# First-group attention in place, log gates summed in the projection, tile 0 routed and chosen before the rest of its group

## The reference, cut to what matters

```python
h = rms_norm(x, norm1_g)
rq, rk, rv, rg, fq, fk, fv, ff = split(h @ w_in)      # 7 groups of 512 columns, 8 gate columns
logf = log_sigmoid(ff + b_f)
ro = retention(rotary(rq), rotary(rk), rv)            # 8 heads of 64
c = cumsum(logf)                                      # along tokens
fo = softmax(fq @ fk.T / 8 + c_q - c_k, causal) @ fv  # 8 heads of 64
x = x + concat(rms(ro) * silu(rg), rms(fo)) @ w_out
# PEER: 8 heads, 2 x 128 keys each, 16 experts of 16384 per head and token
q = rms_norm(x) @ wq
v1, i1 = top_k(q1 @ keys1, 16); v2, i2 = top_k(q2 @ keys2, 16)
cv, ci = top_k(v1[:, None] + v2[None, :], 16)         # 16 x 16 candidates per head
e = i1[ci // 16] * 128 + i2[ci % 16]; g = softmax(cv)
x = x + sum_k g_k * gelu(x . u[e_k]) * v[e_k]         # 128 experts per token, 1024 + 1024 values each
```

## Time and profile before

| | |
|---|---|
| median of three runs | 4024.57 us (4021.61 to 4029.34) |
| the profiled execution's own time | 4017.62 us |
| its span, first to last instruction | 4015.8 us |
| TensorE busy | 2392.5 us (60%) |
| VectorE busy | 2507.4 us (62%) |
| ScalarE busy | 474.8 us (12%) |
| GpSimd busy | 1397.8 us (35%) |
| mean granted TensorE clock | 0.748 |
| gather queue, share of the 16 DMA engines' span | 72.9% (1208.03 MB) |
| all DMA | 1361.03 MB, mean 339 GB/s |

### The profile page before, as it was taken

One profiled execution on the slowest core, in us unless ns is written; L12 is line 12 of the kernel. 1 busy time (PEld: TensorE's weight loads), 2 busy tenths in 40 slices (PEclk: granted clock), 3 DMA queues, 4 the chain that ended last, 5 costly groups with the idle time before them and its releaser, 6 DMA issues.

```text
span 4015.8 us, 34713 instructions
## 1 busy us (share of the span) xinstructions
PE 2392.5 (60%) x11906; PEld 984.7 (25%) x11906; DVE 2507.4 (62%) x6235; ACT 474.8 (12%) x1311; POOL 1397.8 (35%) x1257
## 2 busy tenths in 40 slices
PE   7999867838847665855726746684334334334333
PEld 3456333413313222322402322231001001001000
DVE  3226211789656655888886656689887555555555
ACT  1001121211102201101111211010001000000000
POOL 0001100026434433433343434344444444444443
PEclk9988957969968887876767878796666656556556
DMA  3010342079999998999999999999999999999998
GB/s 112 21 37 22 122 161 100 6 287 418 387 417 419 414 420 360 411 389 409 407 412 418 411 411 420 378 411 412 419 410 419 419 419 418 417 419 418 420 417 371
DMA packets 252929, 1361.03 MB, mean 339 GB/s; under 512 B 33857, under 2 KB 54153, under 8 KB 105297
## 3 DMA queue, kind: packets, MB, share of 16 engines
q0 software_dynamic: 165888, 1208.03, 72.9%
q1 hardware_dynamic: 84560, 148.45, 10.1%
q10 hardware_dynamic: 2304, 2.32, 0.2%
HBM read 1328.37 MB, written 30.35 MB: 338 GB/s over the span
## 4 chain that ended last, share of the span: by engine, by line
DMA 37%; PE 20%; DVE 15%; POOL 7%; issue 6%; ACT 1%; SPq 1%; POOLq 0%; DVEq 0%; ACTq 0%
DMA M<-in_peer_uv,M 35%; PE yp L1952 11%; POOL M L1524 7%; DVE M L2210 6%; PE ab L1905 2%; PE c L1884 1%; DMA M<-qts_scratch 1%; DVE strips L2232 1%; DVE exg L2227 1%; PE d L1768 1%; PE ab L1745 1%; DMA qts_scratch<-M 1%; PE d L1884 1%; PE ef L1940 1%; DVE gel L2219 1%
## 5 line engine op out<-in xcount | busy, mean ns | idle before, releaser
L1524 POOL DMA_INDIRECT M<-in_peer_uv,M x1152 | 1308.9, 1136 | 1937.5 <-PE yp L1952 1499.2
L2210 DVE SCALAR_TENSOR_TENSOR M<-M 128x1024 f32<-128x1024 f32 x1152 | 1410.4, 1225 | 838.7 <-DMA M<-in_peer_uv,M 805.3
L1952 PE MATMUL yp<-M,strips 128*32 128x512 f32 x4608 | 905.4, 927 | 1301.6 <-DVE strips L2232 1263.3
L1952 PEld LDWEIGHTS yp<-M,strips 128*32 128x32 f32 x4608 | 161.3, 145 | 1924.0 <-DVE strips L2232 1509.0
L1706 ACT ACTIVATE gel<-gel 128x4 f32<-128x4 f32 x288 | 59.2, 206 | 2113.1 <-DVE gel L2221 2076.6
L1905 PE MATMUL ab<-M 128*128 128x512 f32 x576 | 263.8, 609 | 1.3 <-ACT M L1662 1.3
L411 PE MATMUL z<-M 128*128 128x512 f32 x432 | 188.4, 593 | 0.9 <-PEq L104 0.9
L1905 PEld LDWEIGHTS ab<-M 128*128 128x128 f32 x576 | 109.1, 196 | 142.3 <-issue 140.7
L1785 PE MATMUL ab<-M 128*128 128x512 f32 x288 | 133.4, 613 | 13.1 <-issue 10.0
L2232 DVE SCALAR_TENSOR_TENSOR strips<-gel,exg 128x128 f32<-128x128 f32 x288 | 84.0, 292 | 59.1 <-ACT gel L1706 49.2
L1745 PE MATMUL ab<-M 64*128 64x512 f32 (+3 forms) x192 | 96.7, 618 | 27.7 <-DMA M<-qts_scratch 22.3
(11 more groups left out here) (232 smaller groups left out, 2578.1 us busy)
## 6 DMA issues: line engine op xcount, KB each, us to landing
M<-in_peer_wq SPq DMA_DIRECT2D x12, 2048.0 KB, 28.1
M<-in_w_in SPq DMA_DIRECT2D x9, 2048.0 KB, 8.6
M<-in_peer_uv,M POOLq DMA_INDIRECT x1152
M<-in_w_out SPq DMA_DIRECT2D x24, 512.0 KB, 25.4
M<-in_x_prompt SPq DMA_DIRECT2D x16, 512.0 KB, 10.2
x_scratch<-M SPq DMA_DIRECT2D x9, 512.0 KB
xts_scratch<-M SPq DMA_DIRECT2D x9, 512.0 KB, 35.9
M<-xts_scratch SPq DMA_DIRECT2D x9, 512.0 KB
```

Of the source, the lines that this page charges most:

```text
L1524: nc.gpsimd.indirect_dma_start(ring[n % NR], None, a["peer_uv"], bass.IndirectOffsetOnAxis(ap=idxH[:, t % 6, s // 4, s % 4:s % 4 + 1], axis=0)
L1952: last = nc.tensor.matmul(yp[32 * j:32 * j + 32, 512 * c:512 * c + 512], strips[:, n % 2, j, :], ring[(4 * n + j) % NR][:, D + 512 * c:D + ...
L2210: nc.vector.scalar_tensor_tensor(out=row, in0=row, scalar=1.0, in1=xrep[:, s % 4, :], op0=ALU.mult, op1=ALU.mult, accum_out=dots[:, t % 2, ...
```

## The change

1. In the second projection the log gates of the prompt are transposed behind step 3 and those of the samples behind step 5; ScalarE copies them at steps 4 and 6, VectorE sums them ahead of step 5, and SyncE stores `csd` and `lft` ahead of step 6. `lgfT`, `ones0` and `csum0` move to parts of the value and key regions that this phase leaves unused.
2. The attention of group 0 reads `qT`, `kT` and `vn` where the projection left them, and the retention outputs where the retention left them; the loads of `kTg`, `vg`, `fq` and `mix` are gone for g = 0. The tail begins with the decay rows of heads 0 and 1.
3. The weights follow later decay rows: w_out's first four chunks behind the row of head 2, the other four behind head 3, wq blocks 0 and 1 behind heads 4 and 5, the routing keys behind head 6.
4. Group 0 routes tile 0 first (i = 0 to 3), then block by block for tiles 1 and 2. In the plan the first top 16 of i = 4 needs tile 0's choice to be complete. Gather 4 waits for `s_mm` 8. The routing keys of group 0 are split in two places, so that blocks 2 and 3 lie outside the ring.
5. The plan's model changes: `rscore` needs the SyncE part of the last `hxt`, which costs 32 us instead of 6 for groups 1 and 2 (the keys are loaded there), and two of three SyncE slots of a tile count as ready four dots later.

```diff
-        lgfT = Hreg[0:NH, 7040:7040 + TILES * P]
+        lgfT = M[0:NH, 28160:28160 + TILES * P]
+        ones0, csum0 = M[0:NH, 29312:29312 + NP_TOK], M[0:NH, 32768:32768 + NP_TOK]
...
+                        if with_ff and n == 6:
+                            sp.wait_ge(c_done, 1)
+                            sp.dma_start(a["csd"], csum0).then_inc(out_done, 16)
+                            sp.wait_ge(ffT, 2)
+                            sp.dma_start(a["lft"], lgfT[:, NP_TOK:]).then_inc(out_done, 16)
+                            outs += 2
...
+                        if with_ff and n == 3:
+                            pe.wait_ge(ff_log, 1)
+                            for u in range(PT):
+                                last = nc.tensor.transpose(ffpt[:, u // 4, (u % 4) * P:(u % 4 + 1) * P], lgf[:, u, :], ident[:, :])
+                            last.then_inc(ft_done, 1)
+                        if with_ff and n == 5:
+                            pe.wait_ge(ffT, 1)
+                            nc.tensor.transpose(ffpt[:, 0, 0:P], lgf[:, ST, :], ident[:, :]).then_inc(ft_done, 1)
...
+                        if with_ff and n == 5:
+                            dve.wait_ge(ones_set, 1)
+                            dve.wait_ge(ffT, 1)
+                            nc.vector.tensor_tensor_scan(out=csum0, data0=ones0, data1=lgfT[:, 0:NP_TOK],
+                                                         initial=0.0, op0=ALU.mult, op1=ALU.add).then_inc(c_done, 1)
...
-                add(rest, ("load", g), sp=(55.0 if g else 12.0, *routed))
-                add(rest, ("loadq", g), sp=(40.0 if g else 15.0, *chosen))
+                add(rest, ("load", g), sp=(55.0 if g else 6.0, *routed))
+                if g:
+                    add(rest, ("loadq", g), sp=(40.0, *chosen))
...
-                            act=(1.4, ("pe", ("hxt", g, j))), sp=(6.0, ("act", ("hxt", g, j))))
+                            act=(1.4, ("pe", ("hxt", g, j))),
+                            sp=(32.0 if g and j == GT - 1 else 6.0, ("act", ("hxt", g, j))))
...
-                            add(rest, ("rscore", g, i), pe=(1.4, ("act", ("rturn", g, i)), *bank("D", "act", ("rscore", g, i))),
+                            add(rest, ("rscore", g, i), pe=(1.4, ("act", ("rturn", g, i)), ("sp", ("hxt", g, GT - 1)),
+                                                              *bank("D", "act", ("rscore", g, i))),
                                 act=(0.7, ("pe", ("rscore", g, i)), *old))
+                        first = [("dve", ("rcand", 0, 0, CAND - 1))] if g == 0 and i == 5 and p == 0 else []
                         if i >= 1:
-                            add(rest, ("rtop", g, i - 1, p), dve=(1.15, ("act", ("rscore", g, i - 1))))
+                            add(rest, ("rtop", g, i - 1, p), dve=(1.15, ("act", ("rscore", g, i - 1)), *first))
...
-                    top = ("rtop", g, 4 * i + 3 if g == 0 else n - GT + i, 4)
+                    top = ("rtop", g, 3 if g == 0 and i == 0 else n - GT + i, 4)
...
-            return (i % 4, i // 4) if g == 0 else (i // GT, i % GT)
+            if g:
+                return i // GT, i % GT
+            return (i, 0) if i < 4 else ((i - 4) // 2, 1 + i % 2)
...
-                need = (P * t - 1, P * t - 1, P * t + 3)[k] if i else -1
+                need = (P * t + 3, P * t + 3, P * t + 3)[k] if i else -1
...
-            keys4 = M[:, 16384:18432].rearrange("p (s i n) -> p s i n", s=4, i=4)
+            keys4 = [M[:, o:o + 1024].rearrange("p (s i n) -> p s i n", s=2, i=4) for o in (16384, 34304)]
...
                     elif kind == "decay":
                         h = arg[0]
                         sp.wait_ge(ttr_done, FIRST[g] + (h - 1) * len(tiles_of(g)))
                         load_decay(NH * g + h)
+                        if g == 0 and h in (2, 3):
+                            load_wout(0, range(4 * h - 8, 4 * h - 4))
+                        elif g == 0 and h in (4, 5):
+                            load_wq(0, h - 4)
+                        elif g == 0 and h == 6:
+                            for b in range(4):
+                                sp.dma_start(keysT(0, b), a["keys_t"][:, 4 * b:4 * b + 4, :]).then_inc(key_in[b], 16)
...
                     if n == 4:
-                        pool.wait_ge(s_mm, 4 * GT)
+                        pool.wait_ge(s_mm, 8)
...
+                    rows_q, rows_k = (fq[:, :, i * P:(i + 1) * P], kTg) if g else (qT[:, :, t * P:(t + 1) * P], kT)
...
-                nc.vector.tensor_tensor_scan(out=csum0, data0=ones0, data1=lgfT0[:, 0:NP_TOK],
-                                             initial=0.0, op0=ALU.mult, op1=ALU.add).then_inc(c_done, 1)
```

More of the change, by code:

```diff
@@ L421, in _ @@
                             turn(n)
[L422 to L430, removed]
                 @block.scalar
@@ L452, in _ @@
                     for n, (g, t) in enumerate(steps):
+                        if with_ff and n == 4:
+                            act.wait_ge(ft_done, 1)
+                            nc.scalar.copy(lgfT[:, 0:NP_TOK], ffpt[:, :, :].rearrange("h a n -> h (a n)")).then_inc(ffT, 1)
+                        if with_ff and n == 6:
+                            act.wait_ge(ft_done, 2)
+                            nc.scalar.copy(lgfT[:, NP_TOK:], ffpt[:, 0, 0:P]).then_inc(ffT, 1)
                         if g in (RV, FV):
@@ L469, in _ @@
                             evacuate(n)
[L470 to L475, removed]
                 @block.gpsimd
@@ L479, in _ @@
                     steps_done = 0
+                    if with_ff:
+                        nc.gpsimd.memset(ones0, 1.0).then_inc(ones_set, 1)
                     for m, n in enumerate(normed):
@@ L910, in fox @@
                         add(rest, ("decay", g, h + 1), sp=(11.0 if g else 2.5, ("dve", ("foxs", g, last))))
-                wait = [("sp", ("load", g)), ("sp", ("loadq", g))] if n == FIRST[g] else []
+                wait = [("sp", ("load", g)), ("sp", ("loadq", g))] if g and n == FIRST[g] else []
                 old = [("act", ("foxs", g, n - 2))] if n - 2 >= FIRST[g] else []
                 free = [("pe", ("foxp", g, n - 3))] if n - 3 >= FIRST[g] else []
-                cb = [("sp", ("decay", g, h))] if h >= 2 else []
+                cb = [("sp", ("decay", g, h) if h >= 2 else ("load", g))]
                 add(rest, ("foxs", g, n),
@@ L1085, in work_ready @@
                         return None
-                    empty = done.get(("pe", ("rscore", 0, 4 * GT - 1)))
+                    empty = done.get(("pe", ("rscore", 0, 7)))
                     if i >= 4 and empty is None:
@@ L1304, in rows, with load_wout @@
                         a[name + "_s"][0].rearrange("b n h d -> (b n) (h d)")
-                def load_wout(g):
-                    for k in range(KC):
+                def load_wout(g, chunks=range(KC)):
+                    for k in chunks:
                         sp.dma_start(wout(g)[:, k, :], a["w_out"][0, k * P:(k + 1) * P, :]).then_inc(w_in[k], 16)
@@ L1444, in load_xTn @@
                     sp.dma_start(xTn.rearrange("p k n -> p (k n)"), a["xts"][t]).then_inc(xTn_in, 16)
-                sp.wait_ge(c_done, 1)
-                sp.dma_start(a["csd"], csum0).then_inc(cs_out, 16)
-                sp.dma_start(a["lft"], lgfT0[:, NP_TOK:]).then_inc(lf_out, 16)
+                for step in due["sp"][0][:1]:
+                    front(step)
                 sp.dma_start(grow[:, :], a["norm2_g"].partition_broadcast(P)
@@ L1452, in _ @@
                 for t in range(TILES):
-                    for step in due["sp"][3 * t]:
+                    for step in due["sp"][3 * t][0 if t else 1:]:
                         front(step)
@@ L1527, in gather @@
                     ).then_inc(uv_in[n % NR], 16)
-                nc.gpsimd.memset(ones0, 1.0).then_inc(ones_set, 1)
                 for n in range(P * TILES):
@@ L1744, in scores @@
                         w = min(512, width - c)
-                        nc.tensor.matmul(s[:, c:c + w], fq[b0:b0 + 64, r, i * P:(i + 1) * P],
-                                         kTg[b0:b0 + 64, r, c:c + w], start=True, stop=c + w < width)
+                        nc.tensor.matmul(s[:, c:c + w], rows_q[b0:b0 + 64, r], rows_k[b0:b0 + 64, r, c:c + w], start=True, stop=c + w < width)
                     nc.tensor.matmul(s[:, t * P:width], identb[:, :], maskq[:, :], start=False, stop=True
@@ L1767, in values @@
                     for j in range(t + 1):
-                        last = nc.tensor.matmul(Dk[b0:b0 + 64, 0:P], vg[:, j, h * HD:(h + 1) * HD], pT[:, n % 2, j, :],
+                        last = nc.tensor.matmul(Dk[b0:b0 + 64, 0:P], (vg if g else vn)[:, j, h * HD:(h + 1) * HD], pT[:, n % 2, j, :],
                                                 start=(j == 0), stop=(j == t))
```

40 lines of the change are left out of this document (15 added, 25 removed).

## The result

The changed kernel takes 3983.09 us (median of four runs, 3978.03 to 3989.30), against 4026.45 us (4021.61 to 4029.34) for the kernel before. The ratio is 0.9897, 95% interval 0.988 to 0.9913: 43 us gained where 75 were forecast. The profiled execution has a span of 3982.5 us and a time of its own of 3984.28 us. The pair of profiled executions differs by 33.3 us only, since that of before lies 8.8 us under its median and that of after 1.2 us above its own. In that of after the phases that the change does not touch also ended 5.1 us later.

The account below looks back on a forecast made before the run. The gather stream on the DMA engines sets the end by its start, bytes and holes. Starting 65 us earlier, plus 18 for holes, less a 7 us wait, makes 76, taken as 75: 4024.6 - 75 = 3950 us, range 3928 to 3982.

Parts of the forecast that it names:

- The projection's end: Second projection, before the tail: early transposes make the last stores about 1.3 us later, bounds 0 to +1.4.
- The attention: Group 0's attention: no wait for queries or late decay rows, ending at 591.4, a gain of 23.5 us, bounds 17 to 25.
- the rival of the high clock: Group 0's attention: TensorE's clock stays high, saving about 25 us more, total 3925 us; chance 0.12.
- Choosing tile 0, and gather 4: Stream start: top 16 tasks moved behind tile 0's choice gain 29.4 us, gather 4 needing score 8 gains 11.8.
- Holes (part 5): First routing scores of groups 1 and 2: the plan's cost fills the waits for keys, gaining 18 us, bounds 0 and 18.
- The holes stay: Rival: the wait for the keys only moves to another step ahead of `add_v`, total 3962 us; chance 0.13.
- A new wait at tile 3: Gather 384, tile 3's first: ready at 1884, numbers at 1891, a wait of 7 us, bounds nothing to 37.
- The prediction's own sum: Start of group 1's front: eight remaining top 16 tasks, slowed by dots from about 777, end at 857.
- the prediction's argument that the choice would run faster: Gather 384: while GpSimd waits, VectorE has no dots, so the choice runs two to three times faster.
- The front of group 1 comes late: Rival: delayed projection of tiles 3 to 8 makes GpSimd wait at gather 384, total 3979 us; chance 0.15.

Follow-up runs that it names:

- Experiment 2: Changed kernel with group 0 routed tile by tile again, no early choice of tile 0, gather 4 waiting for score 12: 4006.47 us, ratio 0.9941.
- Experiment 5: Changed kernel without the early choice of tile 0 in the plan, new routing order and wait for score 8 kept: 4006.34 us, ratio 0.9947.
- Experiment 3: Changed kernel with the plan's new dependency and 32 us cost for the keys undone, SyncE slots kept: 3987.32 us, ratio 0.9898.
- experiment 4: Changed kernel with SyncE issuing the keys of groups 1 and 2 ahead of the last store and of wq block 1: 3963.73 us, ratio 0.9844.
- experiment 1: Changed kernel with tile 3 using tile 2's expert numbers and gates, so its gathers don't wait for its own: 3977.98 us, ratio 0.9877.
- experiment 7: The kernel of experiment 1 with twelve pieces of tile 3's choice left out: 3966.7 us, ratio 0.9843.
- experiment 6: The kernel of experiment 4 with the projection's first 2 MB of weights issued once group 0's last queries are made: 3955.63 us, ratio 0.9817.

## Why the prediction was right up to the stream, and wrong behind it

**The projection's end** was right: from the first of the 128x512 matmuls to the end of the last, 65.5 us before and 66.5 after, +1.0 for a forecast of 1.3.

**The attention** was right in size and in place. The first minimum started 3.1 us after the issue of its decay row (519.41), at net 517.4 (518.2 forecast), there was no later wait for a row, and the last `fout` ended at net 591.4. (The forecast's 591.4 goes back to the start of the last `fout`, 614.91; start against start it is net 590.8.) The clock stayed at its low level as the forecast took it, so the rival of the high clock is out; three windows of after:

```profile
530.00:535.00 5.00, 5.00 (x18) 2.82 (x17) 0.57 (x2) 1.89 (x8) 0.00 (x0) 0.50 0.90 330
560.00:565.00 5.00, 4.65 (x17) 2.96 (x16) 1.04 (x6) 2.26 (x8) 0.00 (x0) 0.50 0.67 174
590.00:595.00 5.00, 4.21 (x17) 2.75 (x17) 0.00 (x0) 1.64 (x5) 0.00 (x0) 0.50 0.02 3
```

Experiment 2 confirms the price by itself: about 22 us.

**Choosing tile 0, and gather 4** were right: choice end net 761.4 (762), gather 0 net 766.4 (767), gather 4 6.3 us behind it (within 7). Experiment 5 measures the early choice alone at 29.4 us of start.

**Failed: "Holes (part 5)".** The 18 us were priced rightly and their cause misread. The step took the wait to be one of order (other work put in its place), so that a larger cost in the plan would fill it. The keys are late because SyncE issues them behind three 0.5 MB stores and behind 4 MB of weights, in a strict order: the first score came 40 us later, and SyncE's issue moved with it, from 1546.42 to 1584.02. The wait went from 11.02 to 11.51 us, a gain of nothing for a forecast of 18. Experiment 3 shows that the cost does nothing to these waits, experiment 4 that a new order on SyncE gives 19 us. So far this is the rival "The holes stay", at its price.

**Failed: "A new wait at tile 3".** The forecast had gather 384 ready at 1884; it would have gone at 1914.55 - 28.69 = 1885.9, net 1880.8. It had tile 3's numbers at 1891; they came at 1910.04 + 4.25 = 1914.3, net 1909.2. An error of 3 and one of 18 us turned a wait of 7 into one of 28.7. The step that broke is the start of the front of group 1, the end of the twelfth top 16, set at 845, "5 us earlier than before", as a point in time. SyncE's first projection weights wait for just that; here they are before and after:

```profile
852.71 0.38 SPq L1319 DMA_DIRECT2D M<-in_w_in  x1
```

```profile
874.65 0.38 SPq L1336 DMA_DIRECT2D M<-in_w_in  x1
```

So the front starts at net 869.6, 25 us later than forecast and 17 later than before. The prediction's own sum had said 857, and it went down to 845 on account of a bound of 832 that the plan came nowhere near. The front stands in fixed order with the stream. Dots that are already done in VectorE's list when each step comes, and its start:

```
step                          before           after
last top 16 of group 0 (i=11) 845.6  (4 dots)  860.9  (33 dots)
first sum of the projection   918.2  (25)      937.7  (56)
first new attention minimum   1176.1 (111)     1205.2 (145)
first top 16 of group 1       1584.0 (252)     1623.6 (288)
choice of tile 3, last piece  1891.2 (357)     1909.3 (384)
```

The last of the eight tasks that were pushed behind tile 0's choice now starts behind 33 dots instead of 4, and the dots take their time from the tasks; by the first top 16 of group 1 the front is 40 us later (34 net). From there to the choice's last piece its list has 96 dots among it where it had 105, and the lag falls to 18 us (13 net). The wait of GpSimd has no part in that, against the prediction's argument that the choice would run faster during it: in experiment 1, which has no such wait, the last piece starts at 1909.1 as well. In stream terms it is simpler: the choice's 27 dots of slack to gather 384 (384 - 357) were all spent, and one gather's share of the stream is about 3 us. In the prediction's list this is the rival "The front of group 1 comes late", whose condition was numbers 25 us later than before; they came 13 us later. What it cost is less than the 28.7 us of the profile: experiments 1 and 7 get back 5 and 16 us, by taking out the wait and then the work too, and experiment 6 gets back 8 with the work in an earlier place. By the windows, the loss is 19.4 us larger than before from 1850 to 2050, 6 larger from 900 to 1550, 5 smaller between and 5 larger from 2050 to 3900: 25 in all, of the 17.7 + 9.3 = 27 of the accounting. (Its cut at gather 384 goes through the middle of the hole near 1900.) Held against the forecast, 38 us are missing: 18 for the holes, 12 for what the place near 1900 costs beyond the 7 foreseen, 6 in the other stretches, and 2 that the windows don't place.

**The two rivals came together.** Alone they stood at 3979 and 3962. Holes that stay cost 18 us, and the late front between nothing and the 22 us by which the wait was longer: 3968 to 3990, measured 3983. With the 12 us of the windows it is 3980. I had added their chances but no case with both, though nothing excludes it, and so the range ended 1 us short.

**Open.** The hole of experiment 5 at 1000 us is read from its trace, and no run takes it away; the one at 1200 us was not followed. Experiments 5 and 6 have the list of all steps changed at once, since the plan is made anew, so neither gives the price of a single place. That the stretch without dots holds up the ring goes by the traces: it lasts 17.7 to 29.0 us behind dot 384 in the five kernels that lose 14.6 to 30.7 us there, and at most 9.1 in before and in experiments 2, 5 and 6, which lose 4.2 to 10.6. But these go together with the place of the choice, and no run breaks up the stretch while it leaves the rest in place. The windows don't place the 11 us of experiment 7 there.

## What to carry to other kernels

When a stream starts earlier and the work for its later parts is dealt in a fixed order among it, count the slack in items of the stream and not in microseconds: the front moved with its dot number, and 27 dots of slack vanished with one reordering. When a wait is gone, look at the stretch that a plan has built around it: without the wait experiment 1 still had 22.7 us without a dot there. Before a wait is "hidden" by a cost in a plan, see who issues the load and what stands ahead of it in that queue; a new order there gave 19 us where the plan gave none. And where two rivals don't exclude each other, the range must hold them both at once.

## What was not expected of the hardware

The time that SyncE needs to issue DMAs depends on what is already queued: three 0.5 MB stores took 19.47 us and two 256 KB key loads 7.72 us at the issue behind two 2 MB blocks, but two stores took 2.64 and the key loads 1.03 us behind one block (experiment 4). The first of the three stores alone took 13.85 us at the issue; in experiment 4 each of the five took 0.3 to 0.4 us. So the order on the queue counted twice, in the transfer and in the issue.

In the attention TensorE was 84 to 100% busy in the windows above and the clock stayed at 0.50 (1.2 GHz) in both kernels. It rose at nearly the same point of the span in both: before, between 610 and 615, still in the attention; after, between 610 and 615 as well, though the attention had ended at 596.5 and TensorE had stood idle from 600 to 605. How busy TensorE was doesn't sort these stretches; what does was not found. After, TensorE alone (busy, clock, DMA share, GB/s):

```profile
600.00:605.00 5.00, 0.00 (x0) 0.50 0.97 378
605.00:610.00 5.00, 1.97 (x8) 0.50 1.05 390
610.00:615.00 5.00, 4.52 (x7) 0.63 0.61 223
615.00:620.00 5.00, 5.00 (x13) 1.00 0.00 0
```
